# Three 256-column matmuls for each weight block, with one copy out of PSUM on VectorE, in place of a 512-column and a 256-column matmul with a copy on ScalarE and an add on VectorE

## The chip, the cores and the metric

The kernel runs on one core of one Trainium2 chip. The metric is the device time of one execution in microseconds; the kernel before took 3724.37 us (median of three runs, 3720.9 to 3728.54).

## The reference, cut to what matters

The program computes four layers on 256 positions of width 2048, in float32: an S5 layer (state space scan) and a FoX attention layer with a shared key and value projection, then two hybrid layers, each with modulation, a retention branch, a latent attention branch and a merge. Nearly all of the arithmetic lies in products with large weights:

```python
xn = rmsnorm(h, g_pre)
uz = xn @ w_in                        # 2048 x 4096
y = y * jax.nn.sigmoid(y @ w_glu + b_glu)
return h + rmsnorm(y @ w_out, g_post)
...
kvf = rmsnorm(h, g_kv) @ w_kv         # 2048 x 4112
qz = rmsnorm(h, g_pre) @ w_in
...
h = rms_norm(x, g_norm) * (1.0 + scale[:, None, :]) + shift[:, None, :]
proj = h @ w_in                       # 2048 x 14400
q = (rms_norm(cq, g_cq) @ w_uq)       # 512 x 3072
kv = (rms_norm(ckv, g_ckv) @ w_ukv)   # 512 x 4096
merged = g_a * y_ret + g_b * y_mla
out = merged @ w_out
```

## The kernel before, in words

Activations lie transposed in SBUF: 128 channels on the partitions, 256 positions (`T`) in the free dimension, 16 such tiles (`KT`) for the width of 2048. A weight matrix is cut into blocks of 2048 x 128: one block is 1 MB, 128 x 2048 values in SBUF, and gives one result tile of 128 x 256. `NBLOCKS` = 483 blocks go by in a fixed order, job after job (`FIRST_JOBS`, `LAYER_JOBS`).

To reach float32 accuracy with the `fp32r` format, each operand is split in two: hi is the value rounded to fp32r and lo is what is left. ScalarE (ACT) writes `whi` (L410), VectorE (DVE) writes `wlo` = `raw` - `whi` (L754). The activations are split likewise into `xs[:, k, 0, :]` (hi, ACT L463) and `xs[:, k, 1, :]` (lo, DVE L818). The product is whi x (xhi and xlo) + wlo x xhi. For each of the 16 k of a block TensorE (PE) issues two matmuls (L1256, L1258): `whi` against the 512 columns of `xs[:, k, :, :]`, which fills a PSUM bank `acc`, xhi's part in columns 0 to 255 and xlo's in 256 to 511, and `wlo` against the 256 columns of xhi, which adds to columns 0 to 255. Each matmul instruction has its own load of weights (LDWEIGHTS, "PEld").

The result is the sum of both halves of `acc`. ACT copies the second half to `acctmp` (L431), and DVE adds the first half and `acctmp` into the destination (L793, counted in `acc_summed`). There are two `acc` banks: PE begins tile t when tile t-2 has been summed. There are 563 result tiles.

The order on each engine is written out by hand and the same for all: for block j, ACT copies the half of tile j and then splits block j+2 (`split_hi`); DVE adds a step of the modulation product where a job carries one (L785), adds tile j, then makes `wlo` of block j+2 (`split_lo`). SP loads `raw` (four buffers) once the `wlo` of its earlier content is done. After each block a `side` function may put in other work: attention, norms, gates. Jobs without side work run in loops of four blocks (`blocks_of`), the others are unrolled.

The jobs `uq` and `ukv` multiply 512 rows only: one block holds four tiles (or two), with 4 k each. Their split goes in pieces, one between two tiles (`hi_piece`, L417; `lo_piece`, L767). `uq` has 6 tiles and `ukv` 8, four times in each of two layers; they come between jobs `gb` whose side work is attention.

Of the kernel before, what the change touches and what calls it, by code (L numbers as in the profile page):

```python
# [7 lines left out]
F32 = mybir.dt.float32  # L8
F32R = mybir.dt.float32r
I32 = mybir.dt.int32  # L10
ALU = mybir.AluOpType
ACT = mybir.ActivationFunctionType
AXX = mybir.AxisListType.X

P = 128
T = 256
# [103 lines left out]
def hybrid_program(nc, x_t, wstream, modstream, vecs, s5_adt, s5_b, s5_c, fox_bf, positions,  # L120
                   eye, rope_inv, rope_swap, masks, decay, out):
    K = 1024
    BASE, TOP = 16512, 229344
    with ExitStack() as ctx:
        used = [BASE]

        def at(name, shape, dt, off):
            assert off + 4 * int(np.prod(shape[1:])) <= TOP, (name, off)
            return nc.alloc_sbuf_tensor_at(name, shape, dt, offset=off)

        def take(nbytes):
            o = used[0]
            used[0] += -(-nbytes // 32) * 32
            assert used[0] <= TOP, used[0]
            return o
# [11 lines left out]
        whi = [at(f"whi{i}", [P, BW], F32R, o_hi + i * 8 * K) for i in range(SPL)]  # L147
        wlo = [at(f"wlo{i}", [P, BW], F32R, o_lo + i * 8 * K) for i in range(SPL)]
# [6 lines left out]
        ones_1 = at("ones_1", [P, 1], F32, take(32))  # L155
        swaps = at("swaps", [P, 2, P], F32, take(1024))
        trig = at("trig", [P, 2, 2, T], F32, take(4 * K))
        acctmp = at("acctmp", [P, 2, T], F32, take(2 * K))
        vec = at("vec", [P, NVEC], F32, take(4 * NVEC))
        modv = [at(f"modv{l}", [P, 48], F32, take(192)) for l in range(2)]  # L160
        cact = at("cact", [P, KT], F32, take(64))
# [44 lines left out]
        acc = [ctx.enter_context(nc.psum_tensor(f"acc{i}", [P, 512], F32)) for i in range(2)]  # L206
# [6 lines left out]
        def sem(name):  # L213
            if name not in sems:
                sems[name] = ctx.enter_context(nc.semaphore(name))
            return sems[name]

        raw_loaded = [sem(f"raw_loaded{i}") for i in range(RAW)]
        mod_loaded = [sem(f"mod_loaded{i}") for i in range(2)]
        (w_hi_done, w_lo_done, acc_done, acc_low_copied, acc_summed, mod_acc, mod_reduced, mod_added,  # L220
         x_staged, x_hi_done, x_lo_done, sq_done, sq_used, ms_ready, ms_rooted, rstd_ready, params_loaded,
         s5_loaded, rope_swapped, rope_done) = map(sem, (
             "w_hi_done", "w_lo_done", "acc_done", "acc_low_copied", "acc_summed", "mod_acc", "mod_reduced",
             "mod_added", "x_staged", "x_hi_done", "x_lo_done", "sq_done", "sq_used", "ms_ready", "ms_rooted",
             "rstd_ready", "params_loaded", "s5_loaded", "rope_swapped", "rope_done"))

# [65 lines left out]
        def tiles_of(key, j, s):  # L292

            b0, t0, nb, per = JOBS[key]
            if per == 1:
                return [(j + t0, s + t0, j, 0)]
            before = sum(per[:s])
            return [(t0 + before + q, t0 + before + q, before + q, q) for q in range(per[s])]

        def split_ahead(key, j):  # L300

            b0, _, nb, _ = JOBS[key]
            return not isinstance(j, int) or (b0 + j + SPL < NBLOCKS and not (key == (None, "z") and j >= nb - SPL))
# [10 lines left out]
        def positive(j, n):  # L314

            return not isinstance(n, int) or n > 0
# [86 lines left out]
        def _(act):  # L403
# [16 lines left out]
            def project(key, side=None):  # L420
                b0 = JOBS[key][0]

                def one(j, s):
                    piece, whole = pieces(key, j)
                    for t, par, _, q in tiles_of(key, j, s):
                        if piece:
                            hi_piece(*piece, q)
                        act.wait_ge(acc_done, t + 1)
                        if positive(j, t - 1):
                            act.wait_ge(acc_summed, t - 1)  # L430
                        act.activation(acctmp[:, par % 2, :], acc[par % 2][:, T:2 * T], ACT.Copy).then_inc(acc_low_copied, 1)  # L431
                    if whole and split_ahead(key, j):

                        split_hi(j + (b0 + SPL), b0 + s + SPL)
                blocks_of(act, key, one, side)

# [87 lines left out]
            for b in range(NTB):  # L524
# [4 lines left out]
                for c in range(16):  # L529
                    r, j, ks = input_chunk(c)  # L530
# [217 lines left out]
        def _(dve):  # L748
# [23 lines left out]
            def project(key, dest, rows=P, side=None):  # L772
                b0 = JOBS[key][0]
                mod = MOD_JOBS.index(key) if key in MOD_JOBS else None
                if mod is not None:
                    if mod:
                        dve.wait_ge(mod_reduced, 4 * mod)
                    dve.memset(modacc[:, :], 0.0).then_inc(mod_acc, 1)

                def one(j, s):  # L780
                    if mod is not None:

                        dve.wait_ge(mod_loaded[s % 2], j * 8 + (8 * (mod * MOD_STEPS - s % 2) + 16))
                        dve.wait_ge(mod_acc, j + (1 + (MOD_STEPS + 1) * mod))
                        dve.scalar_tensor_tensor(out=modacc[:, :], in0=modw[s % 2][:, :],  # L785
                                                 scalar=cact[:, bass.ds(j, 1)] if not isinstance(j, int) else cact[:, j:j + 1],
                                                 in1=modacc[:, :], op0=ALU.mult, op1=ALU.add).then_inc(mod_acc, 1)
                    piece, whole = pieces(key, j)
                    for t, par, jt, q in tiles_of(key, j, s):
                        if piece:  # L790
                            lo_piece(*piece, q)
                        dve.wait_ge(acc_low_copied, t + 1)
                        dve.tensor_tensor(out=dest(jt), in0=acc[par % 2][0:rows, 0:T], in1=acctmp[0:rows, par % 2, :],  # L793
                                          op=ALU.add).then_inc(acc_summed, 1)
                    if whole and split_ahead(key, j):
                        split_lo(j + (b0 + SPL), b0 + s + SPL)
                blocks_of(dve, key, one, side)
                if mod is not None:
                    dve.wait_ge(mod_reduced, 4 * (mod + 1))
                    l, c = divmod(mod, MOD_CHUNKS)  # L800
                    b = VEC_AT[f"b_mod{l}"] + 8 * c
                    dve.tensor_tensor(out=modv[l][:, 8 * c:8 * c + 8], in0=bank[5][:, 0:8], in1=vec[:, b:b + 8],
                                      op=ALU.add).then_inc(mod_added, 1)
                    dve.wait_ge(mod_added, mod + 1)
# [435 lines left out]
        def _(pe):  # L1240
            def project(key, x_split, fresh=None, cols=P, kts=KT, side=None, before_mod=None):


                b0 = JOBS[key][0]

                def one(j, s):
                    pe.wait_ge(w_lo_done, j + (b0 + 1))
                    w = (b0 + s) % SPL
                    for t, par, _, q in tiles_of(key, j, s):
                        if positive(j, t - 1):  # L1250
                            pe.wait_ge(acc_summed, t - 1)
                        for k in range(kts):
                            if fresh and isinstance(j, int) and j == 0 and q == 0 and k % 4 == 0:
                                pe.wait_ge(x_lo_done, SPLIT_BEFORE[fresh] + k // 4 + 1)
                            c = (q * kts + k) * cols
                            pe.matmul(acc[par % 2][0:cols, :], whi[w][:, c:c + cols], x_split[:, k, :, :],  # L1256
                                      start=(k == 0), stop=False, skip_group_check=True)
                            mm = pe.matmul(acc[par % 2][0:cols, 0:T], wlo[w][:, c:c + cols], x_split[:, k, 0, :],  # L1258
                                           start=False, stop=(k == kts - 1), skip_group_check=True)
                        mm.then_inc(acc_done, 1)  # L1260
                blocks_of(pe, key, one, side, fresh)
                if key in MOD_JOBS:

                    mod = MOD_JOBS.index(key)
                    pe.wait_ge(mod_acc, (MOD_STEPS + 1) * (mod + 1))
                    if before_mod:
                        pe.wait_ge(*before_mod)
                    for j in range(MODW // P):
                        for q in range(4):
                            rows = slice(32 * q, 32 * q + 32)  # L1270
                            mm = pe.matmul(bank[5][rows, j:j + 1], modacc[:, j * P + 32 * q:j * P + 32 * q + 32], ones_1[:, :],
                                           start=True, stop=True)
                            if j == MODW // P - 1:
                                mm.then_inc(mod_reduced, 1)
# [58 lines left out]
            for q in range(8):  # L1333
# [3 lines left out]
                for k in range(4):  # L1337
                    src = s5bd[r][:, 4 * (kt + k):4 * (kt + k) + 4, :].rearrange("p a c -> p (a c)")
                    mm = pe.transpose(bank[q % 4][:, k * P:(k + 1) * P], src, ident[:, :])
# [315 lines left out]
```

## Time and profile before

| | |
|---|---|
| median of the runs | 3724.37 us (3720.9 to 3728.54) |
| span of the profiled execution | 3729.7 us |
| PE busy | 3197.5 us, 86% |
| PE weight loads busy | 2750.2 us, 74% |
| DVE busy | 2483.3 us, 67% |
| ACT busy | 1446.9 us, 39% |
| weights and other data from HBM | 628.02 MB |

The profile is of one execution; its span is 5.3 us over the median. Matmul rows give the start of an instruction and a duration that is longer than the distance to the next one, as matmuls overlap in the pipeline; the pace is read from the starts. "PEclk" or "granted clock" is the share of TensorE's full clock that it was granted. An idle time stands in brackets behind the row that it precedes, with the row that ended it. A reader should look first for the engine that is seldom idle, then at what it does most, then at what ends its few waits.

### The profile page before, as it was taken

The page shows a single profiled execution, that of the slowest core. Times are in us where ns is not written, and L with a number is a line of the kernel's source. Part 1 is how long each engine was busy: PE and PEld are TensorE (multiplying, and loading weights), DVE is VectorE, ACT ScalarE, POOL GpSimd, SP SyncE. Part 2 cuts the span into 40 slices and gives each one's busy share as a digit, 9 for nine tenths or more (in the row PEclk, how much of TensorE's full clock was granted, in tenths as well). Part 3 has the DMA queues.
Part 4 walks back from the last instruction along what each step waited for, and adds up shares of the span by engine and source line. Part 5 has one row for each costly group of instructions (what it writes and reads, how often), then busy time and mean ns, then how long its engine had stood idle before and what let it go on. Part 6 is the DMA issues. An engine that isn't in the chain of part 4 may idle for free. (4 is left out here: it accounts for less than half of the span.)

```text
span 3729.7 us, 56483 instructions
## 1 busy us (share of the span) xinstructions
PE 3197.5 (86%) x22836; PEld 2750.2 (74%) x22836; DVE 2483.3 (67%) x3383; ACT 1446.9 (39%) x1764; POOL 133.6 (4%) x218
## 2 busy tenths in 40 slices
PE   7982210997999997999999999998999999999998
PEld 6872210886878876888888777887888888777887
DVE  6449999767776756576777656775565575655564
ACT  4330100443344543333444444344333454444343
POOL 0000000000000000000000000000000000000000
PEclk9975555998999998999999999999999999999999
DMA  5520000765766443566667435764544454434453
GB/s 196 184 78 2 2 1 23 250 240 176 265 236 242 175 148 146 199 248 240 216 237 259 147 125 201 261 253 175 185 177 158 158 215 181 147 125 180 170 192 113
DMA packets 101036, 645.70 MB, mean 173 GB/s; under 512 B 11360, under 2 KB 12000, under 8 KB 36704
## 3 DMA queue, kind: packets, MB, share of 16 engines
q1 hardware_dynamic: 70880, 513.23, 38.2%
q0 software_dynamic: 27648, 100.68, 7.5%
q10 hardware_dynamic: 2304, 28.84, 1.9%
q8 instruction: 157, 2.57, 0.3%
q14 instruction: 47, 0.39, 0.0%
HBM read 628.02 MB, written 14.68 MB: 172 GB/s over the span
## 5 line engine op out<-in xcount | busy, mean ns | idle before, releaser
L1256 PE MATMUL acc<-xs,whi 128*128 128x512 f32 x7216 | 2602.2, 404 | 102.1 <-DVE xs L818 90.2
L1258 PE MATMUL acc<-xs,wlo 128*128 128x256 f32 x7216 | 2037.5, 282 | 0.0
L1256 PEld LDWEIGHTS acc<-xs,whi 128*128 128x128 f32 x7216 | 1371.7, 190 | 444.7 <-issue 96.0
L754 DVE TENSOR_TENSOR wlo<-raw,whi 128x2048 fp32r<-128x2048 f32 x459 | 1051.8, 2292 | 534.2 <-ACT whi L410 534.2
L1258 PEld LDWEIGHTS acc<-xs,wlo 128*128 128x128 f32 x7216 | 1380.5, 191 | 6.0 <-issue 3.6
L410 ACT ACTIVATE whi<-raw 128x2048 fp32r<-128x2048 f32 x459 | 875.0, 1907 | 0.0
L431 ACT ACTIVATE acctmp<-acc 128x256 f32<-128x256 f32 x563 | 215.0, 383 | 1454.8 <-PE acc L1258 1437.8
L793 DVE TENSOR_TENSOR w<-acc,acctmp 128x256 f32<-128x256 f32 (+1 forms) x496 | 209.4, 423 | 526.5 <-ACT acctmp L431 525.3
L785 DVE SCALAR_TENSOR_TENSOR modacc<-modw,cact,modacc 128x1024 f32<-128x1024 f32 x192 | 245.4, 1278 | 12.7 <-DMA modw<-in_modstream 11.2
L389 POOL DMA_DIRECT2D modw<-in_modstream x192 | 101.6, 529 | 1778.7 <-DVE modacc L785 1041.7
L1370 PE MATMUL acc<-state,ct 128*32 128x64 f32 x512 | 10.8, 262 | 152.2 <-DVE state L870 152.2
L870 DVE TENSOR_TENSOR hsame<-abar_same,state 128x128 f32<-128x128 f32 x256 | 99.9, 390 | 39.1 <-ACT state L532 30.2
L1370 PEld LDWEIGHTS acc<-state,ct 128*32 128x32 f32 x512 | 10.3, 140 | 152.8 <-DVE state L870 152.6
L1370 PE MATMUL bank<-state,ct 128*32 128x64 f32 x512 | 12.4, 290 | 124.2 <-DVE state L870 124.2
L1357 PE MATMUL bank<-uslice,bt 32*32 32x64 f32 x4096 | 92.2, 299 | 28.9 <-issue 26.8
L532 ACT ACTIVATE state<-bank 128x512 f32<-128x512 f32 x64 | 38.2, 597 | 202.6 <-PE bank L1357 132.1
L1357 PEld LDWEIGHTS bank<-uslice,bt 32*32 32x32 f32 x4096 | 84.4, 156 | 36.5 <-issue 36.3
L477 ACT ACTIVATE smx<-smx,stat 128x128 f32<-128x128 f32 x96 | 43.0, 448 | 176.0 <-DVE stat L891 176.0
L870 DVE TENSOR_TENSOR hcross<-abar_cross,state 128x128 f32<-128x128 f32 x256 | 104.1, 407 | 0.0
L1370 PEld LDWEIGHTS bank<-state,ct 128*32 128x32 f32 x512 | 12.1, 160 | 124.6 <-DVE state L870 124.6
L870 DVE TENSOR_TENSOR state<-hsame,hcross 128x128 f32<-128x128 f32 x256 | 96.3, 376 | 8.8
L870 DVE TENSOR_TENSOR hsame<-hsame,state 128x128 f32<-128x128 f32 x256 | 101.9, 398 | 0.0
(227 smaller groups left out, 2261.5 us busy)
## 6 DMA issues: line engine op xcount, KB each, us to landing
raw<-in_wstream SPq DMA_DIRECT2D x483, 1024.0 KB, 4.8
modw<-in_modstream POOLq DMA_DIRECT2D x192, 512.0 KB, 4.7
residual<-h ACTq DMA_DIRECT2D x2, 2048.0 KB, 6.3
ga_gate<-w ACTq DMA_DIRECT2D x2, 2048.0 KB, 10.6
gated_retention<-w ACTq DMA_DIRECT2D x2, 2048.0 KB, 8.2
w<-gated_retention ACTq DMA_DIRECT2D x2, 2048.0 KB, 9.3
h<-residual ACTq DMA_DIRECT2D x2, 2048.0 KB, 12.5
w<-ga_gate ACTq DMA_DIRECT2D x2, 2048.0 KB, 10.6
```

What stands on the lines that cost most here:

```text
L389: pool.dma_start(modw[s][:, :], src).then_inc(mod_loaded[s], 16)
L410: act.activation(whi[s % SPL][:, :], raw[slot][:, :], ACT.Copy).then_inc(w_hi_done, 1)
L431: act.activation(acctmp[:, par % 2, :], acc[par % 2][:, T:2 * T], ACT.Copy).then_inc(acc_low_copied, 1)
L477: last = act.activation(smx[:, i % 2, lo:hi], smx[:, i % 2, lo:hi], ACT.Exp, bias=stat[:, i % 2, 2 + n:3 + n], accum_out=stat[:, i % 2, 4 ...
L754: dve.tensor_tensor(out=wlo[s % SPL][:, :], in0=raw[s % RAW][:, :], in1=whi[s % SPL][:, :].bitcast(F32), op=ALU.subtract).then_inc(w_lo_do ...
L785: dve.scalar_tensor_tensor(out=modacc[:, :], in0=modw[s % 2][:, :], scalar=cact[:, bass.ds(j, 1)] if not isinstance(j, int) else cact[:, j ...
L793: dve.tensor_tensor(out=dest(jt), in0=acc[par % 2][0:rows, 0:T], in1=acctmp[0:rows, par % 2, :], op=ALU.add).then_inc(acc_summed, 1)
L870: return dve.tensor_tensor(out=out_, in0=a, in1=b, op=op)
L1256: pe.matmul(acc[par % 2][0:cols, :], whi[w][:, c:c + cols], x_split[:, k, :, :], start=(k == 0), stop=False, skip_group_check=True)
L1258: mm = pe.matmul(acc[par % 2][0:cols, 0:T], wlo[w][:, c:c + cols], x_split[:, k, 0, :], start=False, stop=(k == kts - 1), skip_group_check ...
L1357: mm = pe.matmul(bank[j][32 * q:32 * q + 32, at_k:at_k + TB], bt[r][rows, k, 32 * q:32 * q + 32], uslice[b % 2][rows, k, :], start=True, s ...
L1370: mm = pe.matmul(ybank[b % 2][k // 8][32 * j:32 * j + 32, k % 8 * TB:(k % 8 + 1) * TB], ct[r][:, 4 * k + j, :], state[b % 2][:, r, 4 * k + ...
```

## The change

PE issues three matmuls of 256 columns for each k in place of two: whi x xhi, whi x xlo and wlo x xhi, all accumulated in columns 0 to 255 of the `acc` bank. DVE copies these columns to the destination when PE has finished the tile. ACT's copy, its buffer and its semaphore go. ACT keeps the weight splits: before `split_hi` it waits for the last matmul of the block's last tile, as it did through the copy, and in the pieced jobs it waits once, for the tile before the block, and then makes all the pieces.

```diff
-        acctmp = at("acctmp", [P, 2, T], F32, take(2 * K))
...
                 def one(j, s):
                     piece, whole = pieces(key, j)
-                    for t, par, _, q in tiles_of(key, j, s):
-                        if piece:
+                    tiles = tiles_of(key, j, s)
+                    if piece:
+                        act.wait_ge(acc_done, tiles[0][0])
+                        for q in range(piece[1]):
                             hi_piece(*piece, q)
-                        act.wait_ge(acc_done, t + 1)
-                        if positive(j, t - 1):
-                            act.wait_ge(acc_summed, t - 1)
-                        act.activation(acctmp[:, par % 2, :], acc[par % 2][:, T:2 * T], ACT.Copy).then_inc(acc_low_copied, 1)
                     if whole and split_ahead(key, j):
-
+                        act.wait_ge(acc_done, tiles[-1][0] + 1)
                         split_hi(j + (b0 + SPL), b0 + s + SPL)
...
-                        dve.wait_ge(acc_low_copied, t + 1)
-                        dve.tensor_tensor(out=dest(jt), in0=acc[par % 2][0:rows, 0:T], in1=acctmp[0:rows, par % 2, :],
-                                          op=ALU.add).then_inc(acc_summed, 1)
+                        dve.wait_ge(acc_done, t + 1)
+                        dve.tensor_copy(dest(jt), acc[par % 2][0:rows, 0:T]).then_inc(acc_summed, 1)
...
-                            pe.matmul(acc[par % 2][0:cols, :], whi[w][:, c:c + cols], x_split[:, k, :, :],
-                                      start=(k == 0), stop=False, skip_group_check=True)
-                            mm = pe.matmul(acc[par % 2][0:cols, 0:T], wlo[w][:, c:c + cols], x_split[:, k, 0, :],
-                                           start=False, stop=(k == kts - 1), skip_group_check=True)
+                            a = acc[par % 2][0:cols, 0:T]
+                            pe.matmul(a, whi[w][:, c:c + cols], x_split[:, k, 0, :], start=(k == 0), stop=False)
+                            pe.matmul(a, whi[w][:, c:c + cols], x_split[:, k, 1, :], start=False, stop=False)
+                            mm = pe.matmul(a, wlo[w][:, c:c + cols], x_split[:, k, 0, :], start=False, stop=(k == kts - 1))
```

## Rows read from the trace of the kernel before

**Rows 1.** The page: busy time (share of the span) and instructions of each engine.
```profile
PE 3197.5 (86%) x22836; PEld 2750.2 (74%) x22836; DVE 2483.3 (67%) x3383; ACT 1446.9 (39%) x1764; POOL 133.6 (4%) x218
```
**Rows 2.** Costliest groups of PE: count | busy, mean ns | idle before, releasers.
```profile
L1256 PE MATMUL acc<-xs,whi 128*128 128x512 f32 x7216 | 2602.2, 404 | 102.1 <-DVE xs L818 90.2 <-DVE wlo L754 11.5 <-DVE w L793 0.2
...
L1256 PE MATMUL acc<-cks,whi 128*128 128x512 f32 x256 | 92.4, 404 | 10.8 <-DVE wlo L767 10.8
...
L1256 PE MATMUL acc<-cqs,whi 128*128 128x512 f32 x192 | 79.4, 447 | 19.2 <-DVE w L793 10.3 <-DVE qkv_b L793 9.0
```
**Rows 3.** PE in order of time, 2302 to 2322 us; the window ends: PEclk, DMA, GB/s.
```profile
2302.35 0.28 PE L1258 MATMUL acc<-xs,wlo 128*128 128x256 f32 x1
2302.47 0.40 PE L1256 MATMUL acc<-xs,whi 128*128 128x512 f32 x1
...
2321.79 0.28 PE L1258 MATMUL acc<-xs,wlo 128*128 128x256 f32 x1
2302.00:2322.00 20.00, 20.00 (x115) 17.39 (x114) 11.85 (x10) 10.79 (x10) 2.12 (x4) 1.00 0.88 347
```
**Rows 4.** PE in order of time, 3706 to 3711 us, the last block.
```profile
3706.39 0.28 PE L1258 MATMUL acc<-xs,wlo 128*128 128x256 f32 x1
3706.50 0.39 PE L1256 MATMUL acc<-xs,whi 128*128 128x512 f32 x1
...
3710.89 0.28 PE L1258 MATMUL acc<-xs,wlo 128*128 128x256 f32 x1
```
**Rows 5.** PE in order of time, granted clock 0.50.
```profile
3516.37 0.63 PE L1256 MATMUL acc<-xs,whi 128*128 128x512 f32 x1
...
3517.01 0.63 PE L1256 MATMUL acc<-xs,whi 128*128 128x512 f32 x1
```
**Rows 6.** S5 inputs in order of time, merged rows.
```profile
380.72 2.95 PE L1357 MATMUL bank<-uslice,bt 32*32 32x64 f32 x114 [0.75 <-issue]
```
**Rows 7.** Weight loads of three attention transposes, merged.
```profile
2100.38 0.36 PEld L1314 LDWEIGHTS bank<-ident,smx 128*128 128x128 f32 x3
```
**Rows 8.** Groups of ACT and DVE: the copy, the add, a copy from PSUM.
```profile
L431 ACT ACTIVATE acctmp<-acc 128x256 f32<-128x256 f32 x563 | 215.0, 383 | 1454.8 <-PE acc L1258 1437.8 <-issue 15.9
L793 DVE TENSOR_TENSOR w<-acc,acctmp 128x256 f32<-128x256 f32 x360 | 151.8, 422 | 335.5 <-ACT acctmp L431 334.2
...
L1068 DVE COPY w<-bank 128x256 f32<-128x256 f32 x16 | 6.7, 417 | 2.1 <-PE bank L1324 2.1
```
**Rows 9.** Third tile of a `uq` job, in order of time.
```profile
2104.82 0.41 DVE L870 TENSOR_TENSOR w<-w,bank 128x256 f32<-128x256 f32 x1
...
2105.81 0.65 ACT L431 ACTIVATE acctmp<-acc 128x256 f32<-128x256 f32 x2
2106.22 0.75 DVE L793 TENSOR_TENSOR qkv_b<-acc,acctmp 128x256 f32<-128x256 f32 x2 [0.99 <-ACT acctmp L431]
...
2106.70 0.77 PE L1256 MATMUL acc<-cqs,whi 128*128 128x512 f32 x1 [2.25 <-DVE qkv_b L793]
```
**Rows 10.** Waits of PE before L1256: us in total, times, longest us.
```profile
PE acc L1256 <- DVE xs L818: 90.2, 21, 10.1
...
PE acc L1256 <- DVE wlo L754: 11.5, 11, 3.2
...
PE acc L1256 <- DVE wlo L767: 10.8, 8, 1.4
```
**Rows 11.** Before the start of `retproj`, in order of time.
```profile
3509.16 0.38 ACT L431 ACTIVATE acctmp<-acc 128x256 f32<-128x256 f32 x1 [3.46 <-PE acc L1258]
3509.45 1.90 ACT L410 ACTIVATE whi<-raw 128x2048 fp32r<-128x2048 f32 x1
```
**Rows 12.** DMA by queue (packets, MB, share): S5 inputs, 238 to 283 us.
```profile
q8 instruction: 13, 0.21, 2.1%
```
**Rows 13.** DMA by queue: loop of `k`, 925 to 979 us, all its queues.
```profile
q1 hardware_dynamic: 1356, 9.92, 51.6%
q0 software_dynamic: 1236, 4.47, 21.8%
```

More of the change, by code:

```diff
@@ L219, in hybrid_program @@
         mod_loaded = [sem(f"mod_loaded{i}") for i in range(2)]
-        (w_hi_done, w_lo_done, acc_done, acc_low_copied, acc_summed, mod_acc, mod_reduced, mod_added,
+        (w_hi_done, w_lo_done, acc_done, acc_summed, mod_acc, mod_reduced, mod_added,
          x_staged, x_hi_done, x_lo_done, sq_done, sq_used, ms_ready, ms_rooted, rstd_ready, params_loaded,
          s5_loaded, rope_swapped, rope_done) = map(sem, (
-             "w_hi_done", "w_lo_done", "acc_done", "acc_low_copied", "acc_summed", "mod_acc", "mod_reduced",
+             "w_hi_done", "w_lo_done", "acc_done", "acc_summed", "mod_acc", "mod_reduced",
              "mod_added", "x_staged", "x_hi_done", "x_lo_done", "sq_done", "sq_used", "ms_ready", "ms_rooted",
```

## The prediction

> **What bounds the kernel now.** The shares of busy time come first: TensorE (PE) is busy for 86% of the span of 3729.7 us, the next engine, VectorE (DVE), for 67% [rows 1]. The groups by line say with what. The hi matmuls of 512 columns (L1256) number 7216 + 256 + 192 = 7664, as many lo matmuls of 256 columns (L1258) go with them, and PE's idle time before them is only 102.1 + 10.8 + 19.2 = 132 us [rows 2]. Then the order of time shows what one such k-step costs: from lo to lo it is 19.44 us for 55 steps, 0.353 each, while the DMA engines are busy (share 0.88) [rows 3], and 4.50 us for 13 steps, 0.346 each, in the last block, when nothing is loaded any more [rows 4]. So some 7664 x 0.350 = 2680 us of the span are this one pattern. The S5 scan (about 230 to 650 us) is DVE's and is not touched. The first question is what a k-step costs afterwards, the second which of PE's waits have the removed ACT copy in their chain.
>
> **The k-step: 512 + 256 columns against 256 + 256 + 256.** The columns stay 768. Added are one matmul instruction and one weight load for each k-step, 7664 of each. The page counts 22836 matmuls and as many loads [rows 1], though many matmuls (the norm sums, for one) use the weights of the one before; so the second load of `whi` is not left out.
>
> The cost of "a load and 256 columns" can be read directly, since the present pattern holds it: during the lo matmul of 256 columns the next weights are loaded. From its start to the next hi start it takes 0.12 us [rows 3] or 0.11 us [rows 4] at this resolution; over all 55 and all 13 steps the mean is 0.117 and 0.116. Three such slots are 0.351 and 0.349 us. That is 0.002 less than the step under DMA load and 0.003 more than in the last block. Most stages lie between, and I take the difference as nothing; 3 ns a step either way, 7664 x 0.003 = 23 us, go into the range. At the lower of the clock's two levels (1.2 GHz, granted 0.50) a step takes 0.64 us [rows 5], which is 768 columns at that rate, with nothing added for a load; three matmuls should take the same.
>
> Can PE be fed at that pace? Pairs of load and matmul come every 0.175 us on average now and every 0.117 afterwards. In the S5 inputs 114 pairs take 2.95 us, 0.026 each [rows 6], so issue is far from a limit. Those are small loads; for full ones the nearest row is the attention transposes, three 128 x 128 loads in 0.36 us [rows 7], at most 0.12 each, though in a short burst.
>
> The Trainium skill speaks against the change here. "TensorE: Matmul & The Clock Gate", Part 3, says that a weight load overlaps running matmuls only when its row group differs, and its section on LDWEIGHTS puts a load at the column count over 1.2, or 107 ns. All loads here use all rows; an estimate from that page would be 7664 x 107 ns = 820 us more. The slot of 0.117 us with a load in it disagrees: 256 columns at 2.4 GHz are 0.107 of it, so at most 0.010 us of a load stands bare.
>
> **The way out of PSUM.** Removed are 563 ACT copies of 0.383 us, 215.0 us of ACT time, and the add on DVE, 0.422 us; added is a DVE copy of 128 x 256 out of PSUM, whose like is L1068 at 0.417 us [rows 8]. DVE's time is unchanged (563 x 0.005 = 3 us, hidden). ACT's 215 us lie beside PE's work except where PE waits. DVE's wait moves from the ACT copy to the last matmul, 0.41 us earlier (copy at 2105.81, add at 2106.22 [rows 9]). In the loops a result has a whole tile, 16 x 0.35 = 5.6 us, before its buffer is wanted again, so nothing comes of it there. What counts is PE's waits: 21 behind an `xs` split, 11 behind a `wlo` split, 8 behind a piece of one [rows 10], and those at the `uq` jobs.
>
> (a) Stage changes. The model is the start of `retproj`: after the last matmul ACT copies at 3509.16 and starts the `whi` split at 3509.45 [rows 11]; `wlo`, the `xs` split and PE follow in a chain. Without the copy the chain begins 0.29 us sooner. The first two kinds of wait are 32, of which some are later groups of the same split or behind the S5 work. At least 15 have the copy in their chain, and I take 24: 24 x 0.29 = 7.0 us (4.4 to 9.3).
>
> (b) Tails. After the last tile of `z`, `s5out`, `foxout` and the two `out` the chain runs through copy and add to the next norm or to the scan: 0.41 us, 5 times, 2.1 us.
>
> (c) `uq` jobs, four in each layer. PE waits 2.25 us, until 2106.70, for the result of the first tile. ACT was in its attention work and copied `acc` only at 2105.81, while DVE had ended its own at 2104.82 + 0.41 = 2105.23 and idled for 0.99 us [rows 9]. Afterwards DVE needs no ACT there, and PE starts 0.97 us sooner; the copy before the `whi` split ahead of that attention work goes too, 0.28 more. That is 1.25 us in the three later groups of each layer, 6 x 1.25 = 7.5, and 0.3 in each first group, where DVE itself is late: 8.1 us in all. Next late is DVE's attention work.
>
> (d) `ukv` jobs, 8 times, 10.8 us in all [rows 10]. PE waits for the second piece of `wlo`. Pieces and adds follow one another on DVE without a gap once ACT has begun; ACT begins 0.28 us sooner and runs its second piece at once, but DVE saves only the 0.28: 2.2 us.
>
> (e) Clock. After pauses the steps take 0.64 us for a while [rows 5], 0.29 more than otherwise. If a shorter wait at (c) keeps the level, seven steps or so are saved at each of six places: 0 to 12 us, and I take 3.
>
> SP waits on `w_lo_done`, which comes at most 0.3 us sooner; in the loops nothing asks for that. ACT's new single wait before `split_hi` has only the split behind it, and that had the same wait before. The pieces wait once, for the tile that frees their `whi` slot.
>
> **Sum.** k-steps 0, (a) 7.0, (b) 2.1, (c) 8.1, (d) 2.2, (e) 3: 22.4 us less. The profiled span is 5.3 us over the median of the runs shown; the sum is a difference and comes off both: span 3729.7 - 22.4 = 3707, median 3724.4 - 22.4 = 3702.
>
> **The rivals.** First, slower: three full loads in a row without the long slot of 0.236 us between them, where a backlog of loads may now be worked off. Against it: in the transposes three loads come at no more than 0.12. Its bounds are no effect and the present mean spacing as the least one, 3 x 0.175 = 0.525 a step, 1340 us more. Near the observed slot I price it at 0.120: 7664 x (0.360 - 0.351) = 69 us, so 3771. It decides the sign from a slot of 0.118 on, as 22.4 us over 7664 steps is 3 ns a step. A load that no matmul covers at all would stand beside the 0.107 of columns, which the slot of 0.117 excludes; that form has no more than 0.01 of the chance. (It is the form that the Trainium skill's rule on row groups takes here.)
>
> Second, slower: instruction supply. The loops over four blocks hold 4 x 64 = 256 loads and matmuls on PE now and 384 afterwards. In the S5 inputs 13 instruction packets arrive in 45 us, 3.5 us apart [rows 12], with PE held by "issue" [rows 6]; in the loop of `k` no instruction packet comes in 54 us [rows 13], so the body stays. If the longer one did not, each of 23 backward jumps (2 in `u`, `z`, `glu`, `k`, `q`, 3 in `v`, and in each layer 1 in `rk`, 2 in `mlaproj` and `retproj`) would fetch a packet again: 23 x 3.5 = 80 us, so 3782. The Trainium skill's "Runtime: NRT & Kernel Launch", "Instruction fetch mechanics", has two rules that differ here, a window of two pages of 256 instructions, and room for 2048 on PE; by the first 384 might not fit, by the second they do. The absence of packets fits both.
>
> Third, no change: PE's waits don't shrink, since DVE takes what ACT gives. Then (b) and half of (a) and (d) remain, 7 us: 3717. Against it stand the 0.99 us in which DVE waits for ACT at (c).
>
> **How the numbers follow.** Forecast 0.70, load rival 0.11, supply rival 0.04, no change 0.12, and 0.03 for more (a slot of 0.115 us, 7664 x 0.006 = 46 us less, 3656). A measurement of this kernel can tell about 0.2%, 7 us, from no change. The forecast's own range is the 23 us of the step each way and the bounds of (a) to (e): 3670 to 3731; its upper part lies within 0.2%, so 0.07 of its chance goes to same. Faster 0.63 + 0.03 = 0.66, same 0.12 + 0.07 = 0.19, slower 0.11 + 0.04 = 0.15. The range reaches from 3670 to a slot of about 0.119, 3745, and leaves out most of both slower rivals.
>
> **What would show it.** Three starts per k-step 0.117 us apart, 0.351 in all; 22836 + 7664 = 30500 loads and as many matmuls; no L431, and ACT busy near 1230 us; DVE busy unchanged; at `uq` a wait near 1.0 us in place of 2.25; in the loop of `k` no instruction packets. A slot of 0.120, or a pause at the loops' turns, would make the forecast wrong.

## The result, and the profile after

The changed kernel took 3765.7 us (median of four runs, 3763.61 to 3767.64) against 3722.8 us for the kernel before on the same chip: a ratio of 1.0108, 95% interval [1.0094, 1.0123]. It is 43 us slower by the medians, 40 by the ratio. The forecast was 3702 us and faster; the first rival, slower weight loads, was priced at 3771.

The page of the changed kernel, its busy times (engine, us, share, count) and the groups that answer to [rows 1], [rows 2] and [rows 8]:

```profile
PE 3248.0 (86%) x30500; PEld 3163.2 (84%) x30500; DVE 2479.2 (66%) x3383; ACT 1286.2 (34%) x1201; POOL 133.8 (4%) x218
...
L1253 PE MATMUL acc<-xs,whi 128*128 128x256 f32 x7216 | 2088.0, 289 | 100.2 <-DVE xs L814 90.9
L1254 PE MATMUL acc<-xs,whi 128*128 128x256 f32 x7216 | 2055.2, 285 | 0.0
...
L790 DVE COPY w<-acc 128x256 f32<-128x256 f32 (+1 forms) x496 | 209.7, 423 | 506.4 <-PE acc L1255 506.3
```

The change did what it says: 30500 matmuls and loads, no ACT copy. ACT is at 1286 us and not near 1230: the copy of 0.383 us overlapped the next instruction of ACT, which began 0.29 us after it [rows 11], so 563 copies had been worth 161 us of busy time and not 215. The new thing is in the second entry of the first line: the weight loads (PEld) are busy for 84% of the span, where they were 74% [rows 1].

Now the k-step. PE and its loads in order of time, in a stretch like that of [rows 3]; the columns are start, duration, engine and line:

```profile
2345.36 0.28 PE L1253 MATMUL acc<-xs,whi 128*128 128x256 f32 x1
2345.36 0.19 PEld L1254 LDWEIGHTS acc<-xs,whi 128*128 128x128 f32 x1
2345.48 0.28 PE L1254 MATMUL acc<-xs,whi 128*128 128x256 f32 x1
2345.49 0.19 PEld L1255 LDWEIGHTS acc<-xs,wlo 128*128 128x128 f32 x1
2345.60 0.28 PE L1255 MATMUL acc<-xs,wlo 128*128 128x256 f32 x1
2345.61 0.19 PEld L1253 LDWEIGHTS acc<-xs,whi 128*128 128x128 f32 x1
2345.72 0.28 PE L1253 MATMUL acc<-xs,whi 128*128 128x256 f32 x1
```

In this stretch starts come every 0.12 us: 0.36 us a step. The last block, where nothing is loaded from HBM, has the same pace, unlike before, where the step there was the shortest [rows 4]:

```profile
3739.90 0.28 PE L1253 MATMUL acc<-xs,whi 128*128 128x256 f32 x1
...
3740.98 0.28 PE L1253 MATMUL acc<-xs,whi 128*128 128x256 f32 x1
```

That is 1.08 us for three steps. A pace that is the same with and without traffic, and even from slot to slot, looks like one thing taking its own time. The experiments below test that.

The narrow block `f` gives a control inside the same trace. Its one block has 16 weight columns, so the loads are short (0.09 us instead of 0.19), while the matmuls stream the same 256 columns:

```profile
1084.63 0.28 PE L1255 MATMUL acc<-xs,wlo 128*16 128x256 f32 x1
1084.63 0.09 PEld L1253 LDWEIGHTS acc<-xs,whi 128*16 128x16 f32 x1
...
1085.31 0.28 PE L1255 MATMUL acc<-xs,wlo 128*16 128x256 f32 x1
```

Two steps take 0.68 us there, 0.340 each. Streaming 256 columns takes 0.113 us, then; a slot with a full load takes 0.120.

The waits went as forecast. At the third tile of a `uq` job [rows 9] the changed kernel has

```profile
2124.77 0.41 DVE L866 TENSOR_TENSOR w<-w,bank 128x256 f32<-128x256 f32 x1
...
2125.10 0.75 DVE L790 COPY qkv_b<-acc 128x256 f32<-128x256 f32 x2
```

DVE copies right after its attention work, and PE waits 0.84 us (its row stands below, under the clock) instead of 2.25. The list of waits of PE (us in total, times, longest), against [rows 10]:

```profile
PE acc L1253 <- DVE xs L814: 90.9, 21, 10.1
...
PE acc L1253 <- DVE wlo L751: 9.1, 7, 2.5
...
PE acc L1253 <- DVE wlo L764: 8.0, 8, 1.0
PE acc L1253 <- DVE w L790: 7.0, 4, 3.0
PE acc L1253 <- DVE qkv_b L790: 3.4, 4, 0.8
```

The last two are the waits of the `uq` jobs: 10.4 us together, against 19.2 before [rows 2]. The `xs` waits did not shrink in this view, 90.9 against 90.2 us; the others did, a little.

### The profile page after: what moved, and what is told of

It is laid out like the page before. It is cut to its first block and busy times, and to the rows that moved or that the text cites. A ratio compares the mean times of both kernels' runs of the same rounds, so it can differ in the third digit from the quotient of the medians.

```text
span 3762.5 us, 71062 instructions
## 1 busy us (share of the span) xinstructions
PE 3248.0 (86%) x30500; PEld 3163.2 (84%) x30500; DVE 2479.2 (66%) x3383; ACT 1286.2 (34%) x1201; POOL 133.8 (4%) x218
## 5 line engine op out<-in xcount | busy, mean ns | idle before, releaser
L1253 PE MATMUL acc<-xs,whi 128*128 128x256 f32 x7216 | 2088.0, 289 | 100.2 <-DVE xs L814 90.9
L1254 PE MATMUL acc<-xs,whi 128*128 128x256 f32 x7216 | 2055.2, 285 | 0.0
L1253 PEld LDWEIGHTS acc<-xs,whi 128*128 128x128 f32 x7216 | 1397.3, 194 | 115.0 <-issue 96.7
L1254 PEld LDWEIGHTS acc<-xs,whi 128*128 128x128 f32 x7216 | 1398.0, 194 | 6.3 <-issue 3.6
L1255 PEld LDWEIGHTS acc<-xs,wlo 128*128 128x128 f32 x7216 | 1397.0, 194 | 0.3
L790 DVE COPY w<-acc 128x256 f32<-128x256 f32 (+1 forms) x496 | 209.7, 423 | 506.4 <-PE acc L1255 506.3
```

Source lines behind the costliest of these rows:

```text
L790: dve.tensor_copy(dest(jt), acc[par % 2][0:rows, 0:T]).then_inc(acc_summed, 1)
L1253: pe.matmul(a, whi[w][:, c:c + cols], x_split[:, k, 0, :], start=(k == 0), stop=False)
L1254: pe.matmul(a, whi[w][:, c:c + cols], x_split[:, k, 1, :], start=False, stop=False)
L1255: mm = pe.matmul(a, wlo[w][:, c:c + cols], x_split[:, k, 0, :], start=False, stop=(k == kts - 1))
```

## Experiments

Two theories could explain a slot of 0.120 us: the weight loads follow one another and each takes its own time on its path (load theory), or something else about three equal matmuls costs: the third accumulation into the same PSUM columns, the streaming of columns, or the mere number of matmul instructions. And it was open how much the way out of PSUM gives by itself.

**The matmuls alone.** The kernel before, with its ACT copy and DVE add, and only the matmuls changed:

```diff
-pe.matmul(acc[par % 2][0:cols, :], whi[w][:, c:c + cols], x_split[:, k, :, :], ...)
+pe.matmul(acc[par % 2][0:cols, 0:T], whi[w][:, c:c + cols], x_split[:, k, 0, :], ...)
+pe.matmul(acc[par % 2][0:cols, T:2 * T], whi[w][:, c:c + cols], x_split[:, k, 1, :], ...)
```

> The kernel before with its ACT copy and DVE add, but three 256-column matmuls per k-step; whi x xlo still goes to columns 256 to 511 of the bank. Load theory (each full weight load occupies 0.120 us, three in a row set the step at 0.360 us instead of 0.350): slots of 0.120 us, 7664 x 0.0096 = 73 us more than before, about 3796 us, and no gain from the copy. Rival (it is the third accumulation into the same PSUM columns that costs): slots of 0.114 to 0.117, no change, about 3723 us.

Measured: 3789.9 us, ratio 1.0167 [1.0152, 1.0183], 62 us (57 to 68) more than before. In order of time:

```profile
2345.10 0.28 PE L1256 MATMUL acc<-xs,whi 128*128 128x256 f32 x1
2345.22 0.28 PE L1258 MATMUL acc<-xs,whi 128*128 128x256 f32 x1
...
2345.46 0.28 PE L1256 MATMUL acc<-xs,whi 128*128 128x256 f32 x1
```

The slots are 0.120 although the middle product goes to other columns. The PSUM rival falls. The 62 us are under the 73 that were expected, and the traces say why: in the steps at the upper clock level, some 7100 of the 7664, the mean is 0.3505 us before and 0.3598 here, 0.0093 more, which is 66 us; steps at the lower level pay nothing (0.64 us either way).

The same two kernels also give the price of the way out of PSUM: the changed kernel differs from this one only in that, and its ratio is 1.0108 against 1.0167, 0.0059 x 3725 = 22 us less, some 8 us either way by the two intervals.

**No ACT copy, but two matmuls.** The matmuls of before, ACT and the semaphores of the changed kernel, and one DVE reduce over both halves of the bank:

```diff
-dve.tensor_copy(dest(jt), acc[par % 2][0:rows, 0:T])
+dve.tensor_reduce(dest(jt), acc[par % 2][0:rows, :].rearrange("p (a t) -> p t a", a=2), AXX, ALU.add)
```

> The matmuls of before (512 + 256 columns), but no ACT copy: DVE sums both halves of the bank in one reduce of 512 elements, about 0.68 us in place of 0.42. Load theory: k-step stays 0.350 us; the waits shrink as in the change, which by the difference of 73 us of steps and 43 us measured are worth 30 us; 0.26 us more on DVE for each tail takes a few us back: about 3698 us. Rival (the copy's removal brings nothing, the step grew by less than 73 us): 3723 us or, with DVE's 145 us more, slower.

Measured: 3709.6 us, ratio 0.9953 [0.9939, 0.9968]: faster than before by 17 us, less than the 25 to 30 expected. The page and its DVE group:

```profile
PE 3181.3 (86%) x22836; PEld 2738.6 (74%) x22836; DVE 2626.7 (71%) x3383; ACT 1287.0 (35%) x1201; POOL 133.8 (4%) x218
...
L790 DVE TENSOR_REDUCE w<-acc 128x256 f32<-128x512 f32 (+1 forms) x496 | 342.0, 690 | 437.8 <-PE acc L1255 433.7
```

The reduce costs 0.690 us against 0.423, 0.267 more for each of 563 tiles, 150 us on DVE. Most of it is hidden; the gap between these 17 us and the 22 above is within the intervals.

**A shorter load.** The changed kernel, but the middle matmul loads 64 of the 128 weight columns, so half the rows of its product are left out:

```diff
-pe.matmul(a, whi[w][:, c:c + cols], x_split[:, k, 1, :], ...)
+pe.matmul(acc[par % 2][0:min(cols, 64), 0:T], whi[w][:, c:c + min(cols, 64)], x_split[:, k, 1, :], ...)
```

> The changed kernel, but the second matmul of each k-step (whi x xlo) loads 64 columns of weights and so gives half of its rows; the rest of that product is left out. Its 256 moving columns stay. Load theory: the slot in which the short load runs falls from 0.120 to about 0.114, the others stay: 7664 x 0.006 = 46 us less than the changed kernel, about 3720 us. Rivals (a cost per matmul, of streaming or of PSUM): all slots stay 0.120, 3766 us.

Measured: 3698.5 us, ratio 0.9918 [0.9903, 0.9933]. By the ratios, each to its own runs of the kernel before, that is 71 us less than the changed kernel; the expectation of 46 was short.

```profile
2345.39 0.28 PE L1253 MATMUL acc<-xs,whi 128*128 128x256 f32 x1
2345.39 0.14 PEld L1254 LDWEIGHTS acc<-xs,whi 128*64 128x64 f32 x1
2345.51 0.28 PE L1254 MATMUL acc<-xs,whi 128*64 128x256 f32 x1
...
2345.74 0.28 PE L1253 MATMUL acc<-xs,whi 128*128 128x256 f32 x1
```

The step is 0.35 us with all 768 columns streamed. Halving one load in three took back all that the steps had lost. The gain is not the short load's slot alone: the three slots have medians of 0.117, 0.116 and 0.119 us, each under the 0.120 of the changed kernel.

**Fewer columns.** The changed kernel, but the middle matmul streams 192 columns and, in a second kernel, 64; the product is left out for the other positions. The edit with 192:

```diff
-pe.matmul(a, whi[w][:, c:c + cols], x_split[:, k, 1, :], ...)
+pe.matmul(acc[par % 2][0:cols, 0:192], whi[w][:, c:c + cols], x_split[:, k, 1, 0:192], ...)
```

> The changed kernel, but the second matmul streams 192 columns instead of 256 (the product for 64 positions is left out), with full weight loads. Load theory: the slot after it stays at 0.120, the time is unchanged, 3766 us. Rival (streaming or PSUM writes set the slot): it falls by 64 columns, 0.027 us or more, 7664 x 0.027 = 207 us less, about 3560 us.

Measured: 3697.3 us, ratio 0.9915 [0.9900, 0.9931], 72 us less than the changed kernel by the ratios. The loads in order of time:

```profile
2345.30 0.19 PEld L1254 LDWEIGHTS acc<-xs,whi 128*128 128x128 f32 x1
2345.43 0.19 PEld L1256 LDWEIGHTS acc<-xs,wlo 128*128 128x128 f32 x1
2345.53 0.19 PEld L1253 LDWEIGHTS acc<-xs,whi 128*128 128x128 f32 x1
2345.65 0.19 PEld L1254 LDWEIGHTS acc<-xs,whi 128*128 128x128 f32 x1
```

Neither number was met. Streaming would have given 3560; the load theory, as it was put, no change at all, and there were 72 us. So 0.120 us is not the load's least time, and a second form of the rival arose: each load takes a little from the stream. The next two kernels were made to tell these apart.

> The changed kernel, but the second matmul streams 64 columns instead of 256, with full weight loads; the product whi x xlo is left out for 192 of 256 positions. Load theory (loads follow one another, each holds its path for 0.108 to 0.120 us, a step can't be shorter than its three loads): the step stays near 0.345 us, as with 192 columns, about 3697 us. Rival (a load only takes some 7 ns from the stream, which alone needs 0.113 us for 256 columns): 576 columns 0.255 + 3 x 0.007 = 0.276 us a step, 7664 x 0.084 = 640 us less than the changed kernel, about 3125 us.

Measured: 3709.3 us, 15 under before (ratio 0.9959 [0.9938, 0.9980]), with 576 instead of 768 columns in a step. Matmuls and loads in order of time:

```profile
2345.26 0.28 PE L1253 MATMUL acc<-xs,whi 128*128 128x256 f32 x1
2345.26 0.19 PEld L1254 LDWEIGHTS acc<-xs,whi 128*128 128x128 f32 x1
2345.38 0.19 PE L1254 MATMUL acc<-xs,whi 128*128 128x64 f32 x1
2345.38 0.19 PEld L1256 LDWEIGHTS acc<-xs,wlo 128*128 128x128 f32 x1
2345.41 0.36 PE L1256 MATMUL acc<-xs,wlo 128*128 128x256 f32 x1
2345.49 0.19 PEld L1253 LDWEIGHTS acc<-xs,whi 128*128 128x128 f32 x1
2345.61 0.28 PE L1253 MATMUL acc<-xs,whi 128*128 128x256 f32 x1
```

The matmul after the 64 columns starts 0.03 us later, but the loads start at 2345.26, 2345.38 and 2345.49 as if nothing had changed, and the step is 0.35 (2345.26 to 2345.61). A quarter of the columns gone made the mean step 0.002 us shorter than with 192, 0.347 against 0.349: three loads are the floor, at some 0.116 us each. The whole was even 12 us longer, 16 by the ratios. That lies in the clock: its runs were granted 0.907 to 0.910, those with 192 columns 0.917 to 0.918, and in the traces 268 steps against 191 took the 0.55 to 0.72 us of the lower level, 77 x 0.29 = 22 us, less some 15 us from the shorter steps. Why the clock was granted less was not looked into. Only the last few thousandths, from 0.116 to 0.120, come with full streaming beside them.

**Four loads.** The kernel before with 256 + 128 + 128 + 256 columns, 768 as ever and the result complete:

```diff
-pe.matmul(acc[par % 2][0:cols, :], whi[w][:, c:c + cols], x_split[:, k, :, :], ...)
+pe.matmul(acc[par % 2][0:cols, 0:T], whi[w][:, c:c + cols], x_split[:, k, 0, :], ...)
+for m in range(2):
+    pe.matmul(acc[par % 2][0:cols, T + m * P:T + m * P + P], whi[w][:, c:c + cols],
+              x_split[:, k, 1, m * P:m * P + P], ...)
```

> The kernel before with its copy and add, but four matmuls per k-step: 256, 128, 128 and 256 columns, 768 as ever, complete result. Load theory: four loads of 0.108 to 0.120 us, a step of 0.432 to 0.480 us, 630 to 1000 us more than before, about 4360 to 4730 us. Rival (7 ns from the stream for each load): 0.340 + 4 x 0.007 = 0.368 us, 7664 x 0.018 = 138 us more, about 3865 us.

Measured: 4556.6 us, ratio 1.2238 [1.2212, 1.2263], 831 us more.

```profile
2345.31 0.28 PE L1256 MATMUL acc<-xs,whi 128*128 128x256 f32 x1
...
2345.54 0.19 PEld L1261 LDWEIGHTS acc<-xs,wlo 128*128 128x128 f32 x1
2345.60 0.33 PE L1261 MATMUL acc<-xs,wlo 128*128 128x256 f32 x1
2345.65 0.19 PEld L1256 LDWEIGHTS acc<-xs,whi 128*128 128x128 f32 x1
2345.77 0.28 PE L1256 MATMUL acc<-xs,whi 128*128 128x256 f32 x1
```

A step takes 0.46 us, 4 x 0.115, and 7664 x 0.110 = 843 us. The load theory's 4360 to 4730 holds; the rival's 3865 is out by far. From the third load to the fourth the cost is 0.10 us a step; from the second to the third it was 0.010, since the step of 0.350 with two loads hid nearly all of it.

**The narrow block in every kernel.** Block `f` settles what is left: in each trace it has the same matmul instructions and columns, but loads of 16 weight columns. With four loads, then with 64 columns in the middle matmul:

```profile
1240.34 0.28 PE L1256 MATMUL acc<-xs,whi 128*16 128x256 f32 x1
...
1240.69 0.28 PE L1256 MATMUL acc<-xs,whi 128*16 128x256 f32 x1
```

```profile
1075.24 0.28 PE L1253 MATMUL acc<-xs,whi 128*16 128x256 f32 x1
...
1075.50 0.28 PE L1253 MATMUL acc<-xs,whi 128*16 128x256 f32 x1
```

The step in us at the upper clock level, as the mean of the starts in each trace:

| kernel | loads | columns | loads of 128 columns | loads of 16 (`f`) |
|---|---|---|---|---|
| before | 2 | 768 | 0.350 | 0.347 |
| changed | 3 | 768 | 0.360 | 0.340 |
| 192 in the middle | 3 | 704 | 0.349 | 0.320 |
| 64 in the middle | 3 | 576 | 0.347 | 0.262 |
| four loads | 4 | 768 | 0.463 | 0.354 |

With short loads the step follows the columns, and a fourth matmul costs 0.014 us; with full loads it follows the number of loads. So it is the size of the loads and not the number of instructions that costs. How the floor goes with sizes between 16 and 128 was not run.

**A mixed kernel.** This one follows up the kernel with the reduce. It has the reduce with two matmuls everywhere but in `uq` and `ukv`, which get three matmuls and the plain copy:

> The kernel with the reduce, but the three-matmul form and the plain copy in the jobs uq and ukv (448 of the 7664 k-steps), where DVE's reduce of 0.69 us beside its pieces of 0.69 us for each tile is near PE's 1.4 us. 448 x 0.0096 = 4 us are lost on PE, 16 waits at job starts get 0.32 us shorter, 5 us, and with the clock's share about 3705 us; if DVE is not what holds these jobs, 3713 us. The kernel with the reduce took 3709.6.

Measured: 3702.0 us, ratio 0.9945 [0.9932, 0.9959], 20 us faster than before. It beats the kernel before and the changed one, and lies nearer to the 3705 that was expected than to 3713; from the kernel with the reduce alone (0.9953) the intervals don't tell it apart, though its waits behind `wlo` pieces fell from 10.6 us, 8 times, to

```profile
PE acc L1258 <- DVE wlo L764: 8.0, 8, 1.0
```

## Why the prediction was wrong, point by point

**What bounds the kernel.** Right: PE, and in it the k-step. It was also the reason why a small error there decided the sign.

**The k-step.** This is the step that failed: the cost of "a load and 256 columns" was to be "read directly, since the present pattern holds it", and the term "k-steps 0" came from that. The slot of 0.117 us is real, but it is not the cost in a row of three. Its load could start with the lo matmul because the load before it had had 0.234 us (mean of the trace), twice its need. Two loads of some 0.116 in a step of 0.350 have slack; three have none. In the experiments full loads stand 0.11 to 0.12 apart on average whatever is streamed, and the step is near the larger of two sums: the columns at 0.113 for 256, and the loads at 0.116. Where the two sums lie close (0.340 and 0.348 in the changed kernel) it is some 0.01 above the larger. The term taken as 0 was 62 us by the kernel with the matmuls alone. The bounds "3 ns a step either way" came from the spread of the present step between two stretches (0.353 and 0.346) and not from the question of what else uses the slot. The first rival named the mechanism, the price (a slot of 0.120, 69 us) and the point from which it decides (0.118); it was given 0.11. Its evidence, loads whose rows last 0.19 us in a slot of 0.117, deserved more weight than the transposes, three loads in a row and then a pause. With its 69 us measured as 62, less the 22 us of the waits, the two terms give the 40 us by which the kernel is slower.

The rule of the Trainium skill that was weighed ("TensorE: Matmul & The Clock Gate", Part 3: a load overlaps only with another row group) is not what happens: loads and matmuls overlapped in every kernel here, as at 2345.36 in the changed one, where a load of 0.19 us starts with a matmul of the same rows. But the other number of that page, 107 ns for 128 columns, lies close under the 0.11 to 0.12 us between loads; read as the least distance of loads rather than as time added, it would have given 3 x 0.107 = 0.32 us a step, still under the 0.350 of streaming, so it alone would not have warned.

**The way out of PSUM.** Right in mechanism, and near in its sum: (a) to (e) gave 22.4 us, and the changed kernel against the one with the matmuls alone gives 22 by the ratios (14 to 30) and 24.2 by the profiled executions. These two have the same 30500 matmuls, so their traces can be laid side by side, start by start, and the 24.2 us fall into parts. (c) The third tile of `uq` comes 1.35 us sooner at each of the six places (1.25 was said), and with the two first groups it is 8.5 us where 8.1 was said. (d) The second piece comes 0.27 us sooner in each of the eight `ukv` jobs, 2.1 us where 2.2 was said. (a) The price of a stage change was right, 0.27 us where 0.29 was said, as at `retproj`:

```profile
3514.95 0.77 PE L1256 MATMUL acc<-xs,whi 128*128 128x512 f32 x1 [5.83 <-DVE xs L818]
3543.28 0.55 PE L1253 MATMUL acc<-xs,whi 128*128 128x256 f32 x1 [5.55 <-DVE xs L814]
```

(The first is of the kernel before, the second of the changed one.) But some 14 places show it and not 24. Most do not show it in the list of `xs` waits, because there a wait is counted from PE's last matmul, and that is often one of a norm sum, which moved forward with the rest. Outside `uq` and `ukv` 7 us came off in all, where (a) and (b) had 9.1; (b) can't be told apart in them. (e) The clock was undersized. Where before the steps after the wait of 2.25 us went on at the lower level,

```profile
2107.47 0.63 PE L1256 MATMUL acc<-cqs,whi 128*128 128x512 f32 x1
```

they go on at the upper level in the changed kernel, whose wait is 0.84 us:

```profile
2125.57 0.39 PE L1253 MATMUL acc<-cqs,whi 128*128 128x256 f32 x1 [0.84 <-DVE qkv_b L790]
...
2126.39 0.28 PE L1253 MATMUL acc<-cqs,whi 128*128 128x256 f32 x1
```

In the `uq` jobs 31 steps took the 0.55 to 0.72 us of the lower level before, 20 with the matmuls alone and 5 in the changed kernel: 15 to 26 steps of 0.29 us, 4 to 8 us, where 3 was taken. The mean granted clock in the view of spans by core is 0.916, 0.919 and 0.922. So the sum came out because (e) made up for (a). No part was tried in a kernel of its own. The copy took 0.423 us where 0.417 was taken.

**The supply rival.** No instruction packet comes in the loop of `k` with the longer body either. The DMA queues of the changed kernel, 932 to 986 us, all of them, as in [rows 13]:

```profile
q1 hardware_dynamic: 1328, 9.70, 52.1%
q0 software_dynamic: 1159, 4.22, 20.3%
```

So the body of 384 loads and matmuls stays. The Trainium skill's "Runtime: NRT & Kernel Launch" ("Instruction fetch mechanics") gives PE room for 2048 instructions, and the trace agrees. Its window of two pages of 256 instructions is not excluded by it, since 384 are fewer than 512.

**No change.** DVE did not take what ACT gave: the copy came right after the attention work.

## What to carry to other kernels

Count weight loads per output block as a resource of their own, beside the streamed columns: the step is near the larger of the two sums, and a load that is free while there are two becomes the bound at three. A duration read from a mixed pattern holds in that pattern only; before repeating it back to back, ask which neighbour's slack it lived on. And a result in two halves of a PSUM bank can be summed by one DVE reduce, which freed ACT here without a further load and made the kernel 0.5% faster than before.

## What the runs showed that was not expected

Loads of 128 columns in this format follow one another at 0.11 to 0.12 us in these steps; with full streaming beside them they settle at 0.120, with 192 or 64 columns in one of three matmuls near 0.116. The 0.116 is not a least time everywhere: the full loads of the attention transposes [rows 7], with 128 columns streamed beside them, stand 0.108 us apart in the trace before; those are loads of plain float32 for a transpose, and whether the format or the columns make the difference was not tried. Streaming with short loads runs at 0.113 us for 256 columns (the narrow block), not at the 0.107 that 2.4 GHz gives. Why both are somewhat longer together than apart was not tried. And with the same 768 columns and short loads, two matmuls of 512 and 256 columns take 0.347 us, more than the 0.340 of three of 256; no run tells why.
